# Other start positions for the 272-column tiles, and last queries from the tiles ahead of the norm

## What is computed

```python
def _short_conv_mixer(u, w_in, w_conv, w_out):
    proj = u @ w_in                                   # 1024 -> 4 x 2048
    b_gate, c_gate, xin, z = jnp.split(proj, 4, axis=-1)
    y = depthwise_conv(c_gate * xin, w_conv)          # 3 taps along the tokens
    return (jax.nn.silu(z) * b_gate * y) @ w_out      # 2048 -> 1024

def _mlstm_mixer(u, w_in, gate_b, head_norm_w, w_out):
    proj = u @ w_in      # q, k: 1024 each; v, o, z: 2048 each; 8 gates
    ...

for i in range(2):
    u = _rmsnorm(h, norm_w[i])
    h = h + (_short_conv_mixer if i == 0 else _mlstm_mixer)(u, ...)
```

## Time and profile before

| | us |
|---|---|
| median of three runs | 933.8 |
| span of the profiled execution, first to last instruction | 931.7 |
| PE busy in it | 918.4 |
| DVE busy | 657.8 |
| ACT busy | 533.8 |
| POOL busy | 120.7 |

### The profile page before, as it was taken

How to read it: one execution, slowest core, us unless ns; L and a number is a source line. 1 busy time by engine, 2 the same in 40 slices (tenths; PEclk the granted TensorE clock), 3 DMA queues, 4 the chain that set the end, 5 groups by cost and what they waited for, 6 DMA issues and landing times.

```text
span 931.7 us, 19171 instructions
## 1 busy us (share of the span) xinstructions
PE 918.4 (99%) x7014; PEld 855.9 (92%) x7014; DVE 657.8 (71%) x1115; ACT 533.8 (57%) x902; POOL 120.7 (13%) x111
## 2 busy tenths in 40 slices
PE   7999999999999999999999999999999999999997
PEld 7998889998999998889999999999999998888886
DVE  4898867545899997447877777766667475776743
ACT  6867676545776675446444444444564567676643
POOL 2200010000056663000111111111010000000000
PEclk9999999999999999999999999999999999999999
DMA  8843335435345555553555555555455354444561
GB/s 292 285 163 135 119 108 165 157 118 186 126 165 197 202 203 194 199 194 108 187 178 179 174 175 176 176 182 181 158 182 197 121 179 139 151 143 161 179 201 48
DMA packets 45075, 157.91 MB, mean 169 GB/s; under 512 B 6067, under 2 KB 7219, under 8 KB 44764
## 3 DMA queue, kind: packets, MB, share of 16 engines
q1 hardware_dynamic: 44524, 155.56, 48.7%
q0 software_dynamic: 496, 1.59, 0.5%
HBM read 156.06 MB, written 1.06 MB: 169 GB/s over the span
## 4 chain that ended last, share of the span: by engine, by line
PE 92%; DVE 4%; ACT 2%; issue 1%; DMA 1%; SPq 0%; DVEq 0%; ACTq 0%
PE acc L1240 13%; PE acc L1241 12%; PE acc L1242 12%; PE scores L1240 6%; PE scores L1242 5%; PE scores L1241 5%; PE acc L1195 4%; PE acc L1193 4%; PE acc L1194 4%; PE scores L1195 2%; PE scores L1193 2%; PE scores L1194 2%; PE outs L1194 2%; PE outs L1193 2%; PE outs L1195 2%; PE acc L1315 1%
## 5 line engine op out<-in xcount | busy, mean ns | idle before, releaser
L1795 DVE TENSOR_TENSOR w_lo<-raw,w_hi 128x1024 fp32r<-128x1024 f32 x288 | 354.1, 1235 | 100.4 <-ACT w_hi L604 99.9
L604 ACT ACTIVATE w_hi<-raw 128x1024 fp32r<-128x1024 f32 x288 | 302.4, 1056 | 154.7 <-PE acc L1242 65.5
L1240 PE MATMUL acc<-XH,w_hi 128*128 128x256 f32 (+1 forms) x624 | 178.3, 286 | 0.7 <-DVE XL L1901 0.7
L1241 PE MATMUL acc<-XL,w_hi 128*128 128x256 f32 (+1 forms) x624 | 175.8, 282 | 0.0
L1242 PE MATMUL acc<-XH,w_lo 128*128 128x256 f32 (+1 forms) x624 | 175.8, 282 | 0.0
L1240 PEld LDWEIGHTS acc<-XH,w_hi 128*128 128x128 f32 x624 | 117.4, 188 | 3.2 <-issue 2.6
L1240 PE MATMUL scores<-XH,w_hi 128*128 128x272 f32 (+1 forms) x424 | 120.2, 283 | 0.0
L1242 PE MATMUL scores<-XH,w_lo 128*128 128x272 f32 (+1 forms) x424 | 119.7, 282 | 0.0
L1241 PE MATMUL scores<-XL,w_hi 128*128 128x272 f32 (+1 forms) x424 | 119.7, 282 | 0.0
L1241 PEld LDWEIGHTS acc<-XL,w_hi 128*128 128x128 f32 x624 | 117.5, 188 | 0.1
L1242 PEld LDWEIGHTS acc<-XH,w_lo 128*128 128x128 f32 x624 | 117.3, 188 | 0.0
(11 more groups left out here) (526 smaller groups left out, 1779.3 us busy)
## 6 DMA issues: line engine op xcount, KB each, us to landing
raw<-weights SPq DMA_DIRECT2D x288, 512.0 KB, 3.3
cst<-params SPq DMA_DIRECT2D x1, 1080.5 KB, 9.4
XR<-x_t SPq DMA_DIRECT2D x2, 512.0 KB, 6.5
Y<-mem_t SPq DMA_DIRECT2D x1, 1024.0 KB, 8.1
AR<-bias_rows POOLq DMA_DIRECT2D x4, 256.0 KB, 5.7
out<-AR SPq DMA_DIRECT2D x2, 512.0 KB, 2.6
AR<-final_gain POOLq DMA_DIRECT2D x1, 512.0 KB, 7.0
cst<-params SPq DMA_DIRECT2D x1, 114.5 KB, 3.2
```

Of the source, the lines that this page charges most:

```text
L604: nc.scalar.activation(w_hi[:, n % SLOTS, :], raw[:, n % SLOTS, :], ACT.Copy).then_inc(hi_ready, 1)
L1240: nc.tensor.matmul(o, wh, h, start=start, stop=False)
L1241: nc.tensor.matmul(o, wh, l, start=False, stop=False)
L1795: V.tensor_tensor(w_lo[:, s, :], raw[:, s, :], w_hi[:, s, :].bitcast(F32), ALU.subtract).then_inc(lo_ready, 1)
```

## The change

The 272-column tiles get start positions of their own: LONG_EDGE = 32 for XH and XL (conv_in, lgates, lk), CONV_EDGE = 16 for the 16 tiles of conv_out's input in AH and AL. The 256-column tiles and the normalised tiles of `l_in` stay at 48. The queries of the last layer are multiplied from XH and XL, with the 16 meta columns skipped (position 32 + 16), in place of the normalised tiles, and VectorE multiplies by rstd when it writes them out, in the same instruction as the scale. Since SQ is overwritten there, VectorE first waits until ScalarE and GpSimd have read SQ. TensorE's wait `h1_ready` moves from lq to lv.

```diff
+LONG_EDGE, CONV_EDGE = 32, 16
...
-            at = EDGE + k * (S if w == S else PITCH)
+            at = EDGE + k * S if w == S else CONV_EDGE + k * PITCH
             return slice(at, at + w) if isinstance(k, int) else bass.ds(at, w)
...
+        def x_cols(lo):
+
+            at = LONG_EDGE if lo == 0 else X_EDGE
+            return slice(at, at + T - lo)
...
-                        nc.scalar.activation(XH[:, j, X_EDGE:X_EDGE + T - lo], XR[:, j, lo:T], ACT.Copy, scale=col(gain, j)).then_inc(raw_hi, 1)
+                        nc.scalar.activation(XH[:, j, x_cols(lo)], XR[:, j, lo:T], ACT.Copy, scale=col(gain, j)).then_inc(raw_hi, 1)
...
-                nc.scalar.activation(XH[:, m, X_EDGE:X_EDGE + T], XR[:, m, :], ACT.Copy, scale=col("g_mlstm", m)).then_inc(raw_hi, 1)
+                nc.scalar.activation(XH[:, m, x_cols(0)], XR[:, m, :], ACT.Copy, scale=col("g_mlstm", m)).then_inc(raw_hi, 1)
...
             def xha(k):
-                return XH[:, k, X_EDGE:X_EDGE + T]
+                return XH[:, k, x_cols(0)]
...
             def xla(k):
-                return XL[:, k, X_EDGE:X_EDGE + T]
+                return XL[:, k, x_cols(0)]
...
+            x_tokens = slice(LONG_EDGE + META, LONG_EDGE + T)
             for m in range(KT):
-                chunk(CHUNK["lq"] + m, TILE["lq"] + m, l_in(AH, META), l_in(AL, META), S, ready=h1_ready if m == 0 else None)
+                chunk(CHUNK["lq"] + m, TILE["lq"] + m, lambda k: XH[:, k, x_tokens], lambda k: XL[:, k, x_tokens], S)
...
-                chunk(CHUNK["lv"] + m, TILE["lv"] + m, l_in(AH, 0), l_in(AL, 0), T)
+                chunk(CHUNK["lv"] + m, TILE["lv"] + m, l_in(AH, 0), l_in(AL, 0), T, ready=h1_ready if m == 0 else None)
...
-                V.scalar_tensor_tensor(out=XL[:, k, X_EDGE:X_EDGE + T - a], in0=XR[:, k, a:T], scalar=col(gain, k),
-                                       in1=XH[:, k, X_EDGE:X_EDGE + T - a].bitcast(F32), op0=ALU.mult, op1=ALU.subtract).then_inc(raw_lo, 1)
+                V.scalar_tensor_tensor(out=XL[:, k, x_cols(a)], in0=XR[:, k, a:T], scalar=col(gain, k),
+                                       in1=XH[:, k, x_cols(a)].bitcast(F32), op0=ALU.mult, op1=ALU.subtract).then_inc(raw_lo, 1)
...
+                if m == 0:
+                    dve.wait_ge(normed_hi, 2 * KT)
+                    dve.wait_ge(rest_pool, KT // 2)
                 wait_chunk(dve, n)
-                freed(V.tensor_scalar(lq[:, m, :], acc(t)[:, 0:S], S ** -0.5, None, ALU.mult), t)
+                freed(V.scalar_tensor_tensor(out=lq[:, m, :], in0=acc(t)[:, 0:S], scalar=S ** -0.5, in1=rstd[:, META:T],
+                                             op0=ALU.mult, op1=ALU.mult), t)
```

More of the change, by code:

```diff
@@ L427, in wait_rstd @@
             eng.wait_ge(rstd_ready, (NORM_X, NORM_X1, NORM_X2, NORM_H0, NORM_H1).index(e) + 1)
-        def raw_parts(lo):
-            return (lambda k: XH[:, k, X_EDGE:X_EDGE + T - lo]), (lambda k: XL[:, k, X_EDGE:X_EDGE + T - lo])
+        def x_cols(lo):
+            at = LONG_EDGE if lo == 0 else X_EDGE
+            return slice(at, at + T - lo)
         def l_in(part, lo):
```

## The result

The changed kernel takes 939.6 us (median of 4, 939.17 to 943.21) against 934.05 us before (median of 4, 933.68 to 935.1). The ratio over all runs is 1.0068, with an interval of 1.0056 to 1.0080; by the medians alone it is 1.006. The profiled execution took 939.17 us, of which 937.4 us are the span: 5.7 us more than in the earlier trace rows. The forecast was 925.8 us with a range of 924.3 to 935.5, so it was wrong in its sign.

What follows compares the result with a forecast made beforehand. PE at full clock was taken as the bound, time being the sum of matmul steps. Part 1's 7.1 us and part 2's 0.9 made 8.0 us, taking 933.8 to 925.8 us; range 924.3 to 935.5.

Steps and rivals of the forecast that it cites:

- What bounds the kernel: Whole kernel: PE on 92% of the span at full clock, so time is the sum of distances between matmul starts.
- part 1: 272-column tiles in conv_in, lgates, lk, conv_out moved to 32 and 16: 2136 matmuls from 123.33 to 120.0 ns, 7.1 us gained.
- the fit: Matmul steps: 16 cycles above the columns, plus 8 for each end, first or last, on a 256-byte boundary.
- Part 2: Last queries read XH and XL at 48: 192 matmuls gain 1.3 us (fast pace) or 0.4 (slow); 0.9 us taken.
- Part 3: Work on other engines: query write-out with rstd and DVE's new wait at the first query cost nothing; 3.2 us of slack.
- the cover: conv_in: DVE's waits for PE and the weight queue's spare time suffice for shorter steps, so nothing else becomes the bound.
- Rival 2: XH and XL at 32 meet the weight loads: 304 cycles, 5.8 us lost, conv_out gains 1.3, queries 0.9; 937.4 us, chance 0.15.
- Rival 3: 272-column matmuls: the 24 extra cycles belong to the width, so only the queries gain; 932.9 us, chance 0.12.
- rival 4: 272-column tiles: only one tensor gains, XH alone 927.1 us or AH alone 931.6; chance 0.10.
- Rival 1: conv_in, conv_out, lk: a slow pace after the spread of rstd, 124.5 ns for 2016 steps; 935.2 us, chance 0.11.

Runs made afterwards that it cites:

- e5: Changed kernel with conv_in, gates and keys at 40, conv_out and queries at 56, first block at 8, memory tiles at 40; 938.79 us (before 934.05).
- e2: Changed kernel with conv_in, gates and keys at 0, conv_out at 32, queries at 16, first block at 32, memory tiles at 48; 944.65 us (before 934.0).
- e12: Changed kernel with 32 unused floats behind the weights' buffers, moving only activations; conv_in at 16, conv_out, gates and keys at 48; 943.92 us (before 933.64).
- e4: Changed kernel with 32 unused floats ahead of the weights' buffers, moving weights and activations together; conv_in at 48, conv_out at 16; 934.36 us (before 934.0).
- e1: Changed kernel with conv_in and conv_out back at 48, gates and keys at 32, queries at 48; 933.61 us against 934.0 before, ratio 0.9998.
- e15: Changed kernel with conv_in at 28, conv_out at 4, gates and keys at 20, queries at 36, first block at 20, memory tiles at 4; 942.83 us (before 933.73).

## Why the prediction was wrong, by its steps

- **What bounds the kernel** held: PE, at full clock, and the end is the sum of the steps. So did the count of 2136 matmuls: 2136 x 3.33 ns, with the sign turned, is the loss.
- **The step that failed is part 1**, the value of 120.0 ns for 272 columns off the boundary. Six rows, with three widths and start positions 48, 0 and 16, were fitted by two numbers, 16 cycles and 8, and the one thing that was to be read from the fit, 272 columns at another position, was in none of them. The runs put 304 cycles in its place at 16 and at 32. The upper bound of the same part, 126.7 ns and 7.1 us lost, was the measured value; the text took the lower end because "no end is on the boundary", which is the fit again and no row of its own. With that bound and the queries' 1.3 us the sum is 933.8 + 7.1 - 1.3 = 939.6 us, the measured time.
- **One of the six rows was misread.** In the earlier trace rows the moving operand is not MH at 16: `acc<-w_hi,ML` names the moving one first, as in the earlier trace rows. It is w_hi, from 0 in two pieces of 128 columns, over a stationary tile at 16. So its ends lie on the supposed boundary, and the fit would ask for 288 cycles or more; the row has 272. Read rightly, the rows already spoke against the fit, and of the two that the new positions were likened to, only the earlier trace rows has no end on the boundary. Relative to the stationary tile this row lies at 0 - 16 = 48, as the earlier trace rows does. The expectation of e5 repeats the error with 16 extra cycles for 256 columns at 16; e2 and e12 show 26.7.
- **Part 2** had the right mechanism; the size was at the upper end of its two values. The queries run at the fast pace, 113.5 ns: 1.3 us gained, not 0.9.
- **Part 3 and the cover** held: no idle time of DVE for ScalarE or GpSimd at the first query, 0.42 us for the new form, no new wait of PE. That PE was slower here only widened DVE's cover, so it was not put to a harder test.
- **Rival 2** (position 32 meets the weight loads, slower) gave 304 cycles for XH, the right size, from the row of 22 matmuls at 290 cycles. It gave 937.4 us and had a chance of 0.15. It missed by 2.2 us, since it let conv_out gain 1.3 us at 16, where the runs show a loss of 384 x 3.33 = 1.3. That the weights take part is shown by e4 and e12; in which way the two reads meet is not.
- **Rival 3** (no effect of the position on 272 columns) is refuted too: 296 to 304 cycles by position alone. So is **rival 4** (one of the two tensors gains): neither does.
- **Rival 1** (a slow pace) made none of the difference here, but is real for 272 columns (below).
- The range ended at 935.5 and left out rival 2, the only case in which a whole tensor loses. Part 1's own bounds reached from 7.1 us gained to 7.1 us lost, and no row decided between them, so both belonged in the range.

The Trainium skill, "SBUF — State Buffer", section "SBUF: two separate sides", has TensorE on ports of its own, where it never waits for the other engines. The runs don't contradict that: conv_in's loop keeps one step from start to end while VectorE, ScalarE and GpSimd work beside it. But TensorE's own two streams, the moving tile and the next weights, cost up to 8 cycles a step more or less by how they lie to each other, and the rule names no such cost.

## What to carry over

Where the time is a sum of steps, read the step of the very width, position and neighbour that the change will make; if no row has it, the sign of the effect is as open as its two bounds leave it. In a row of the profile, look up first which operand is the moving one. Where, as here, 128 x 128 fp32r weights are loaded beside every matmul, the start of the moving tile relative to the weight tile modulo 256 bytes is a parameter of the kernel: try it on the chip, stage by stage, and again after anything that moves one of them. For 272 columns here it is worth up to 8 cycles of 304 (2.6%), for 256 columns up to 16 of 288.

## What the runs showed of the hardware that was not expected

- The cost of a matmul beside a weight load depends on the relative position of the two in the row, and takes values between as well: from 272 over 280, 282.7 and 284.8 to 288 for 256 columns, from 296 over 298.7 and 300.8 to 304 for 272.
- From 240 columns down to 192 there is a floor of 268 cycles (111.7 ns) for such a pair; 192 columns cost what 240 do.
- 272 columns have a second pace at one position as well. The 70 steps ahead of the spread (L1145) at position 48 took 123.4 ns before and 126.7 ns in the profiled execution of e1, whose spread is followed by 123.3 ns again; e15 did the same at 28. The rows of e1, with 70 steps between them:

```profile
427.19 0.29 PE L1257 MATMUL acc<-XH,w_lo 128*128 128x272 f32 x1
...
436.06 0.29 PE L1262 MATMUL scores<-XL,w_hi 128*128 128x272 f32 x1
```

- What chooses the pace that a stage enters stays open. It costs little here: 70 steps at 3.3 ns are 0.2 us. So the map above is of the long stages, each of which keeps one pace from its start to its end. At 48, conv_in's loop took 296 cycles in the kernel before, in e1 and in e4; at 32, 304 in the changed kernel, and conv_out at 16 took 304 there and in e4.
- That profiled execution of e1 took 937.65 us against the median of 933.61, and its conv_in began 4.5 us later than in the kernel before (427.19 against 422.65 for the same matmul). That isn't the pace but the clock. TensorE stood idle for 1.29 us, waiting for ScalarE, and in that idle time the granted clock fell; from 56 to 62 us it was 0.50 of full, the lower of its two levels (1.2 GHz). The first products after the idle time, in e1's timeline of PE:

```profile
55.86 0.40 PE L1419 MATMUL outs<-ident,AR 24*128 24x24 f32 x2 [1.29 <-ACT AR L762]
```

Windows of e1: from and to, length, busy time of PE, PEld, DVE, ACT and POOL (instructions in brackets), granted clock, DMA share, GB/s.

```profile
54.00:56.00 2.00, 0.71 (x8) 0.60 (x7) 2.00 (x5) 0.61 (x2) 0.00 (x0) 0.86 0.75 262
56.00:62.00 6.00, 6.00 (x30) 5.30 (x31) 4.93 (x13) 2.66 (x10) 0.00 (x0) 0.50 0.27 87
```

The same six microseconds of the kernel before:

```profile
56.00:62.00 6.00, 5.78 (x48) 5.57 (x48) 5.72 (x17) 2.29 (x10) 0.00 (x0) 1.00 0.29 91
```

With the idle time, this stretch accounts for 4.1 of the 4.5 us; the mean clock of that execution is 0.996, against 0.998 to 1.0 in the others of e1. The changed kernel's slowest run (943.21 us, 0.997) may be the same, but it has no trace. So one profiled execution can be 4 us off the median: where a difference of this size counts, look at the steps and the granted clock, and not at the span alone.
